# Three of eight x columns loaded as exchanged 32x32 blocks and turned by VectorE, in a hybrid attention block on one core

## The reference

```python
h = rmsnorm(x, g_pre_mix)                   # x / rms(x) over features, times g
proj = h @ w_in + b_in                      # 1024 x 2304: aq ak av bq bk bv
out_a = mixer_a(...)                        # window attention, learned sinks, T5 bias
out_b = mixer_b(...)                        # chunk attention, relative bias
y = concat(out_a, out_b) @ w_out
x = x + rmsnorm(y, g_post_mix)
h = rmsnorm(x, g_pre_mlp)
x = x + rmsnorm(square(relu(h @ w_up)) @ w_down, g_post_mlp)
```

## Time and profile before

| what | value |
|---|---|
| median of 3 runs | 1037.31 us (1037.2 to 1037.35) |
| the profiled execution | 1037.82 us |
| its span in the profile | 1036.0 us |
| PE busy | 1026.4 us, 99% of the span |
| DVE, ACT, POOL busy | 771.1, 467.8, 214.9 us |
| granted PE clock, mean | 0.998 |
| DMA | 147.92 MB, mean 143 GB/s |

### The profile page before, as it was taken

The page is one execution under the profiler, slowest core; times in us unless marked ns, Lnnn a source line. Parts: engine busy times, 40 slices in busy tenths (PEclk is TensorE's granted clock), DMA queues, the critical chain, the costliest instruction groups (busy, mean ns, idle before and its releaser), DMA issues.

```text
span 1036.0 us, 15823 instructions
## 1 busy us (share of the span) xinstructions
PE 1026.4 (99%) x5555; PEld 854.0 (82%) x5555; DVE 771.1 (74%) x1505; ACT 467.8 (45%) x961; POOL 214.9 (21%) x200
## 2 busy tenths in 40 slices
PE   9999999999999999999999999999999999999997
PEld 7899887788777888888888888888888888888886
DVE  5855678766679478889988788786444777778997
ACT  5532255554478477846131121221344444444562
POOL 0400000000000003148676675672100000000000
PEclk9999999999999999999999999999999999999999
DMA  9454552110062365135444434436777733454344
GB/s 250 118 134 131 120 134 62 49 65 22 27 183 84 101 184 163 41 127 208 173 168 158 170 128 160 163 133 215 252 240 240 242 95 99 138 193 142 97 139 167
DMA packets 123894, 147.92 MB, mean 143 GB/s; under 512 B 56976, under 2 KB 74264, under 8 KB 121768
## 3 DMA queue, kind: packets, MB, share of 16 engines
q1 hardware_dynamic: 123128, 146.71, 44.8%
q10 hardware_dynamic: 688, 0.20, 0.1%
HBM read 103.65 MB, written 47.49 MB: 146 GB/s over the span
## 4 chain that ended last, share of the span: by engine, by line
PE 96%; issue 1%; DVE 1%; ACT 1%; DMA 0%; SPq 0%; DVEq 0%; ACTq 0%
PE ps L2163 28%; PE ps L2165 28%; PE ps L2164 28%; PE ps L2376 3%; PE ps L2362 2%; PE ps L2343 2%; PE ps L2287 1%; PE ps L2322 1%; PE ps L2495 1%; PE ps L2497 1%; PE ps L2483 1%; PE ps L2175 1%; DMA xraw<-in_x 0%; PE ps L2513 0%; PE ps L2300 0%
## 5 line engine op out<-in xcount | busy, mean ns | idle before, releaser
L2164 PE MATMUL ps<-tm_lo,sm_hi 128*128 128x512 f32 (+1 forms) x450 | 174.6, 388 | 0.0
L2165 PE MATMUL ps<-tm_hi,sm_lo 128*128 128x512 f32 (+1 forms) x450 | 174.6, 388 | 0.0
L2163 PE MATMUL ps<-tm_hi,sm_hi 128*128 128x512 f32 (+1 forms) x450 | 174.6, 388 | 0.0
L2163 PE MATMUL ps<-b_hi,wc_hi 128*128 128x512 f32 x448 | 174.6, 390 | 0.0
L2165 PE MATMUL ps<-b_hi,wc_lo 128*128 128x512 f32 x448 | 174.3, 389 | 0.0
L2164 PE MATMUL ps<-b_lo,wc_hi 128*128 128x512 f32 x448 | 174.3, 389 | 0.0
L1419 ACT ACTIVATE sm_hi<-sm_raw 128x512 fp32r<-128x512 f32 x112 | 70.7, 631 | 162.0 <-DMA sm_raw<-u_matrices 162.0
L2067 DVE TENSOR_TENSOR sm_lo<-sm_raw,sm_hi 128x512 fp32r<-128x512 f32 x112 | 77.7, 693 | 78.3 <-ACT sm_hi L1419 77.7
L2165 PEld LDWEIGHTS ps<-tm_hi,sm_lo 128*128 128x128 f32 x450 | 84.5, 188 | 17.5
L2163 PEld LDWEIGHTS ps<-tm_hi,sm_hi 128*128 128x128 f32 x450 | 84.5, 188 | 17.5
L2163 PEld LDWEIGHTS ps<-b_hi,wc_hi 128*128 128x128 f32 x448 | 84.1, 188 | 17.8 <-DVE wc_lo L1839 0.3
(11 more groups left out here) (239 smaller groups left out, 2062.4 us busy)
## 6 DMA issues: line engine op xcount, KB each, us to landing
u_matrices<-stage SPq DMA_DIRECT2D x112, 256.0 KB, 2.0
sm_raw<-u_matrices SPq DMA_DIRECT2D x112, 256.0 KB, 2.6
up_raw<-in_w_up SPq DMA_DIRECT2D x16, 1024.0 KB, 5.0
w<-in_w_down SPq DMA_DIRECT2D x64, 256.0 KB, 3.7
w_raw<-in_w_in SPq DMA_DIRECT2D x8, 512.0 KB, 3.4
xr<-in_x SPq DMA_DIRECT2D x8, 512.0 KB, 4.7
x_rows<-xr SPq DMA_DIRECT2D x8, 512.0 KB, 5.5
xf<-x_rows SPq DMA_DIRECT2D x8, 512.0 KB, 3.5
```

The source lines that it names most:

```text
L2163: pe.matmul(out, w_hi_, x_hi_, start=start, stop=False)
L2164: pe.matmul(out, w_hi_, x_lo_, start=False, stop=False)
L2165: return pe.matmul(out, w_lo_, x_hi_, start=False, stop=stop)
```

## The change

Columns 5, 6 and 7 (`EXCHANGED`) are no longer turned by PE. SP loads each as 4096 pieces of 32 floats (128 bytes) in four DMAs, which put each 32x32 block at the place that it has when turned; DVE's transpose turns within the blocks, and gives `x_turned` in SBUF. ACT and DVE make `x_hi` and `x_lo` from that. Since the squares need tokens on partitions, the three columns are loaded a second time as rows of 384 features (`x_rows`, two DMAs).

ACT now sums the squares itself, with `accum_out`, in 8 pieces of 128x640 and 8 of 128x384; DVE's adds and its reduction go, one small add comes. Of the eight `rcols` pieces ACT makes four. ACT's high halves of the value weights all come after the columns. The value biases are loaded with their partitions, turned by DVE on a 128x32 tile, and stored in four small DMAs.

```diff
@@ DVE
-                    nc.vector.scalar_tensor_tensor(out=x_lo[:, k], in0=two(6), scalar=g1[:, k:k + 1],
+                    nc.vector.scalar_tensor_tensor(out=x_lo[:, k], in0=column(k), scalar=g1[:, k:k + 1],
...
-                    first_lo(k)
-                for n in ADDED[k]:
-                    add_squares(n)
+                    if k < EXCHANGED[0]:
+                        first_lo(k)
+                if k + 1 in EXCHANGED:
+                    dve.wait_ge(*blocks_landed(k + 1))
+                    nc.vector.transpose(x_turned[k + 1][:], x_blocks[k + 1][:]).then_inc(s_xt, 1)
+                    first_lo(k + 1)
                 if k == KT - 2:
-                    dve.wait_ge(s_acc, KT - 1)
-                    nc.vector.tensor_reduce(out=ss1, in_=sumsq[:], axis=mybir.AxisListType.X, op=ALU.add).then_inc(s_ss1, 1)
+                    dve.wait_ge(s_sq, 2 * T)
+                    nc.vector.tensor_tensor(ss1, ss1, ya1, ALU.add).then_inc(s_ss1, 1)
...
-                    for t in range(T):
+                    for t in range(T // 2):
...
+            dve.wait_ge(s_bv, 17)
+            nc.vector.transpose(bv_rows[:], bv_cols[:]).then_inc(s_bv, 1)
             value_lo(3)
...
-            dve.wait_ge(s_bv, 32)
+            dve.wait_ge(s_bv, 98)
@@ ACT
-SQUARES = ((0, 1), (2,), (3,), (4,), (5, 6), (7,), (), ())
+SQUARED = ((), (), (), (0, 1, 2, 3, 4), (5, 6, 7), (8, 9, 10, 11, 12), (13, 14, 15), ())
+SPLIT_WITH = ((), (1,), (2,), (3,), (4, 5), (6, 7), (), ())
+VALUES_WITH = ((5,), (6, 7), (), (), (), ())
...
+                    nc.scalar.activation(sq[:, n % 2], xraw[:, :, t], ACT.Square, accum_out=ss1[:, t:t + 1]).then_inc(s_sq, 1)
...
+                if k == KT - 1:
+                    act.wait_ge(s_ch1, 1 + STEP)
+                    for t in range(T // 2, T):
+                        last = nc.scalar.activation(rcols[:, t * P:(t + 1) * P], ones[:], ACT.Copy, scale=rs1[:, t:t + 1])
@@ PE
-                if k + 1 < KT:
+                if k + 1 < EXCHANGED[0]:
                     x_transposes(k + 1)
-                else:
-                    pe.wait_ge(s_xlo, column_done(k))
-                    pe.wait_ge(s_rcol, 1)
+                elif k == KT - 1:
+                    pe.wait_ge(s_xlo, column_done(EXCHANGED[0] - 1))
+                    pe.wait_ge(s_rcol, 2)
@@ SP
+            def load_x_blocks(k):
+                rows = x[:, k * P:(k + 1) * P].rearrange("(c j) (a i) -> a j c i", j=32, i=32)
+                for a in range(4):
+                    sp.dma_start(x_blocks[k][32 * a:32 * a + 32].rearrange("j (c i) -> j c i", i=32), rows[a]
+                                 ).then_inc(blocks_landed(k)[0], 16)
...
             load_first_weights(sp, 2)
-            for k in range(4, KT):
-                load_x(k)
+            load_x(4)
+            load_x_blocks(5)
+            for h in range(2):
+                load_x_rows(h)
+            sp.wait_ge(s_xhi, 1)
+            sp.wait_ge(s_xlo, 1)
+            load_x_blocks(6)
+            sp.wait_ge(s_xt, 2)
+            sp.wait_ge(s_sq, 1)
+            load_x_blocks(7)
             sp.dma_start(relrow[:, 0:513], rel).then_inc(s_tab, 16)
             sp.dma_start(t5row[:], t5).then_inc(s_tab, 16)
-            for k in range(5):
-                load_values(k)
+            load_values(0)
+            load_values(1)
...
-            sp.dma_start(vrow.rearrange("a p -> p a"), b_in[:, AV:AV + 5], allow_slow_non_contiguous=True).then_inc(s_bv, 16)
-            sp.wait_ge(s_xt, column_done(KT - 1))
-            sp.wait_ge(s_sq, KT)
+            for k in range(2, 5):
+                load_values(k)
+            sp.wait_ge(s_bv, 1)
+            sp.dma_start(bv_cols[:, 0:5], b_in[:, AV:AV + 5]).then_inc(s_bv, 16)
+            sp.wait_ge(s_xt, column_done(EXCHANGED[0] - 1))
+            sp.wait_ge(s_sq, 2 * T)
...
-            sp.wait_ge(s_bv, 16)
-            sp.dma_start(bv[:], bass.AP(vrow.tensor, 0, [[0, P], [1, VW]])).then_inc(s_bv, 16)
+            sp.wait_ge(s_bv, 18)
+            for g in range(4):
+                sp.dma_start(vrow[:, 32 * g:32 * g + 32], bv_rows[32 * g:32 * g + 5]).then_inc(s_bv, 16)
             sp.wait_ge(s_rowst, 32)
             sp.dma_start(a_rep, bass.AP(bdram.tensor, 0, [[LA + LB, 8], [0, P], [1, LA]])).then_inc(s_rep, 16)
+            sp.wait_ge(s_bv, 82)
+            sp.dma_start(bv[:], bass.AP(vrow.tensor, 0, [[0, P], [1, VW]])).then_inc(s_bv, 16)
             load_fill(0)
```

More of the change, by code:

```diff
@@ L386, in two, with blocks_landed, column @@
             return ps[:, b:b + 2, :].rearrange("p b n -> p (b n)")
+        def blocks_landed(k):
+            return {5: (s_xb, 64), 6: (s_g1, 16 + 64), 7: (s_x0, 16 + 64)}[k]
+        def column(k):
+            return x_turned[k][:] if k in EXCHANGED else two(6)
         def load_first_weights(eng, g):
@@ L502, in build @@
         s_xt = sem("x_columns_transposed")
+        s_xb = sem("x_blocks_landed")
         s_xhi = sem("x_hi_ready")
@@ L1033, in _, with square_rows @@
             nc.scalar.activation(spare[:, 2:3], epsc, ACT.Sqrt)
[L1035 to L1042 removed]
+            def square_rows(n):
+                t = n % T
+                if n == 0:
+                    for k in range(KX):
+                        act.wait_ge(s_in[k], 16)
+                    act.wait_ge(s_x0, 16)
+                elif n >= T and t % (T // 2) == 0:
+                    act.wait_ge(s_in[KX + t // (T // 2)], 16)
+                if n >= 2:
+                    act.wait_ge(s_sq, n - 1)
+                if n < T:
+                    nc.scalar.activation(sq[:, n % 2], xraw[:, :, t], ACT.Square, accum_out=ss1[:, t:t + 1]).then_inc(s_sq, 1)
+                else:
+                    nc.scalar.activation(sq[:, n % 2, 0:KT - KX], x_rows[:, t], ACT.Square, accum_out=ya1[:, t:t + 1]
+                                         ).then_inc(s_sq, 1)
             def value_hi(k):
@@ L1063, in _ @@
                     act.wait_ge(s_xt, column_done(k))
-                    nc.scalar.activation(x_hi[:, k], two(6), ACT.Copy, scale=g1[:, k:k + 1]).then_inc(s_xhi, 1)
-                if k:
-                    first_hi(k)
+                    nc.scalar.activation(x_hi[:, k], column(k), ACT.Copy, scale=g1[:, k:k + 1]).then_inc(s_xhi, 1)
+                for j in SPLIT_WITH[k]:
+                    first_hi(j)
+                for n in SQUARED[k]:
+                    square_rows(n)
                 if k == KT - 2:
@@ L1553, in _ @@
             for i in range(2 * FIRST_TILES):
-                if i < 3:
-                    value_lo(5 + i)
+                for k in VALUES_WITH[i]:
+                    value_lo(k)
                 tile_lo(i)
```

59 lines of the change are left out of this document (27 added, 32 removed).

## The result

The changed kernel takes 1039.67 us in the median of 9 runs (1036.99 to 1040.49), the kernel before in the same session 1037.31 (9 runs). The ratio is 1.0019, 95% interval [1.0010, 1.0027]: about 2 us slower, on the edge of what the prediction called no change. The forecast of 1037.8 with its range of 1035.2 to 1041.0 holds the time. The spread of this kernel is 3.5 us; that of before is 2.3, and 0.5 without one execution.

The account below looks back on a forecast made before the run. PE bounds the kernel: 2.6 us of transposes go, 0.3 is lost to near misses, and the remaining 2.3 us lead meets a 2.8 us wait for `bv`; +0.5 on 1037.3 gives 1037.8 us, range 1035.2 to 1041.0.

Parts of the forecast that it names:

- what the prediction called no change: Whole kernel: a time within 0.2% (2.1 us) of before, the wait for `bv` eating the gain; chance 0.66.
- The gain: PE in the front: 24 transposes go, 3 x 0.87 = 2.6 us less.
- The near misses of DVE and ACT in columns 6 and 7, 0.3 us: Front: x_lo and `rcols` inputs ready about when PE wants them or slightly late; 0.3 us charged, 2.3 of the gain remaining.
- ACT's value weights now come behind column 7: Value products: ACT takes 0.65 us per weight, PE 0.9 per k, so the weights stay ahead of PE.
- The DMA stream 9.2 us longer: SP's queue: block columns and x rows delay everything behind them by 9.2 us, so POOL starts at 34.5.
- the 3.2 us for a block column: DMA in the front: each column of 4096 pieces of 128 bytes takes 3.2 us, against 1.8 for a plain column.
- the slow-blocks rival: DMA in the front: a block column takes 4.4 us, POOL starts at 38.1, kernel at 1041.4 us; chance 0.21.
- POOL's rows, 13.0 us: Bias rows on POOL: 12.3 us before plus 0.7 for DVE operations with two SBUF inputs; rows ready at 47.5.
- `bv` behind the copies: SP's queue: `bv`, issued near 50.8, lands just behind the bias copies at 61.9; PE waits 2.8 us, until 63.5.
- the rival in which the gain survives: `bv` does not queue behind the copies, lands near 53, PE never waits; kernel at 1035.0 us; chance 0.13.
- PE idle from 60.7 to 63.5, released by `v_tok`: Sign on PE before its filling work: a wait for the value biases; without it the forecast is wrong.
- Later stages have not lost any slack that they use.: After the front: masks and first scores come 3.6 us later on DVE, but PE's first weighting of values stands 37 groups behind.

Follow-up runs that it names:

- e8: e5 with the two loads of the tables ahead of x's second block column; 1039.66 us, ratio 1.0018 to the kernel before.
- e9: e8 with the nine loads of constants issued on ScalarE's queue and not SP's; 1035.95 us, ratio 0.9986 to the kernel before.
- e11: The changed kernel with the nine loads of constants issued on ScalarE's queue; 1042.11 us, ratio 1.0044 to the kernel before.
- e12: e9 with the two table loads back behind x's third block column; 1039.40 us, ratio 1.0020 to the kernel before.
- e1: The changed kernel with DVE's turn of the value biases behind the low halves of value weights 3 and 4; 1041.96 us, ratio 1.0039 to before.
- e2: The changed kernel with the bias columns loaded right behind the tables, ahead of the value weights; 1039.65 us, ratio 1.0025 to the kernel before.
- e6: The changed kernel with the loads of value weights 2 to 4 ahead of the nine constants; 1041.57 us, ratio 1.0036 to the kernel before.
- e4: The changed kernel with value biases loaded behind the tables, turned and stored early, bv loaded ahead of the copies; 1039.08 us, ratio 1.0015 to before.
- e5: e4 with the loads of value weights 2 to 4 ahead of the nine constants; 1039.77 us, ratio 1.0022 to the kernel before.
- e3: The changed kernel with value biases stored element by element as before, ahead of the value weights, nothing turned on DVE; 1045.97 us, ratio 1.0082 to before.

## Why the prediction was right, and where it wasn't

- **The gain.** 24 transposes are worth 2.6 us on PE: right. In e8, e9 and e11, where PE waits for nothing in the front, its lead at the value products is 2.9 to 3.0 us. (Some tenths of that are the earlier start of these executions.)
- **The near misses of DVE and ACT in columns 6 and 7, 0.3 us.** DVE did wait, 0.47 us for the blocks of column 6 at 30.19 (forecast to land at 30.5), but PE didn't: it has no wait from 8 to 44 us and reaches `rcols` with all 2.7 us. The term did not show.
- **"ACT's value weights now come behind column 7, 0.65 each, but PE takes 0.9 for each k of the value products, so that they stay ahead."** This is the step that failed. It costed ACT's work and not the arrival of its data. The weights 2 to 4 were moved in SP's program behind the blocks and nine constants and were issued 15 us later, and 5 to 7 stand behind them; ACT waited 2.07 us, DVE 1.84 and then 2.25 for the bias columns, and PE 1.9 us and more, with a stretch at the lower clock behind it. The rule that all that a moved step issues counts on its queue was applied to the tables and not to the weights.
- **The DMA stream 9.2 us longer.** POOL started at 34.04, forecast 34.5: 8.8 us later than before, so the 3.2 us for a block column was near enough, and the slow-blocks rival is out. The 15.3 us that the twelve block loads held SP are this stream seen from the queue, for the most part, and not a cost on top of it.
- **POOL's rows, 13.0 us.** The same 33 operations took 11.8 us in the changed kernel (34.04 to 45.80), 13.8 in e11 and 15.0 in e12; DVE operations with two SBUF inputs run beside them for 4.6, 8.8 and 10.2 us. One operation shows it alone: POOL's 18th took 0.20 us in the kernel before, beside an `x_lo` that read PSUM, and 1.23 us in the changed kernel, beside an `x_lo` of 1.27 us that read SBUF. The Trainium skill (SBUF — State Buffer, the two separate sides) says that a VectorE operation with two SBUF inputs and a GpSimd operation that reads SBUF exclude each other for whole instructions; these numbers agree. The row's time in the changed kernel is short because DVE was waiting, not because the term was too large.
- **`bv` behind the copies.** Right as a mechanism: issued at 48.69, DVE had it at 59.99, 11.3 us later; e1, e2, e6 and e11 show PE waiting for it (1.59, 0.81, 2.64, 4.37 us), e4 shows it gone when `bv` is put ahead. In the changed kernel itself it binds DVE (1.40 us) and not PE, which had already lost its lead. So the rival in which the gain survives is out, but the forecast's own sign, "PE idle from 60.7 to 63.5, released by `v_tok`", wasn't there either. By its own test the forecast was wrong in its place: two limits stood one behind the other, and I had found the second. That PE began its filling work at 63.62, as forecast for 63.5, is luck: in the changed kernel `bv` came at 59.99, 1.9 us sooner than forecast, and three value halves (1.47 us in e11) would be done by 61.5, an estimate, 1.5 us before PE of the kernel before begins its filling work (62.97). Where DVE and PE stand less, PE's wait ends at 63.58 to 64.49 (e1, e2, e6, e11), and these runs bear its size out. The median, 1.9 us above the forecast, is within the range by the range's width, not by this mechanism.
- **"Later stages have not lost any slack that they use."** Wrong for a kernel with its lead, as e5, e8 and e12 show (3 to 4.5 us lost from 85 to 140 us), and without visible effect in the profiled execution of the changed kernel, whose PE was late itself. It was argued from PE's program alone; the exchanges are paced by SP's queue.

What stays open: the median of the changed kernel is 2.4 us above that of before, while its profiled execution explains 0.8. Executions of it differ by 3.5 us. Small shifts of landing times, more or less of the low clock, or a loss after 85 us could each make that; of the executions without a profile only the mean clock is known. It is 0.999 in the two quickest and 0.997 to 0.998 in the rest, which would fit one or two more stretches of low clock in the slower ones (3.4 us at 0.58 is 0.0014 of the mean), but the profiled one, third quickest, has 0.997 too.

## What to carry to other kernels

A load that is moved back in a queue must be followed to its reader, each load, and so must the loads that it pushes back in turn. All that stands ahead counts: twelve loads in small pieces held SP for 15 us while the DMA engines were busy, and nine tiny ones took a steady 0.43 to 0.60 us each, 5 us in all. When a step frees time on the engine that bounds the kernel, list every stream that must now be early by as much, here the weights, the biases, the table copies and the exchanges; the gain is that of the least of them, and removing one wait alone can make the kernel slower (e11 clearly, e1 and e6 by their medians). In e9 four moves together (value weights first, biases early, tables ahead of the second block column, nine small loads on ACT's queue) turned a loss of 2 us into a gain of 1.4; that it needs the last two is shown by e12 and e8.

## What was unexpected of the hardware

- A store in 640 pieces of 4 bytes held up the queue behind it for some 9 us (e3: six issues took 13.04 us against 3.8, and the first weight reached ACT 8.7 us later than in the changed kernel). Behind work that isn't urgent it is free, as it was before.
- A load of 640 numbers, `bv_cols`, issued at 39.67, ended DVE's wait at 45.6: 5.9 us. In e6, where fewer value weights stood just ahead of it, the same load took 2.8 us (41.37 to 44.21). That the weights ahead make the difference is likely and not shown.
- Copies of 1.5 MB within memory hold what is issued behind them for 11.3 us (`bv`), although in e11 the DMA share from 44 to 60 us is 0.40.
- The granted clock fell to the 1.2 GHz level for 3.4 us or so behind PE's waits of 1 to 4 us in some executions (the changed kernel, e6, e11) and not in others with waits of the same size (e1, e2, e4: 1.00 in all windows of 4 us from 44 to 72 us). In the changed kernel PE had stood for 1.03 us at most at a time before the fall. How much of the spread between executions it makes is not shown.
- SP's time to issue a load is no constant: loads of 128 KB in 128-byte pieces, all of one shape, took it 0.43 to 4.16 us each (changed kernel, 14 to 31 us, DMA engines busy), the small constants 0.43 to 0.60 us.
